# Two-layer decoder trunk in split float32: the layer loop written out, the first loads reordered, the position table written from 8 rows

## The reference

```
h = h + 0.5 * swiglu(rms_norm(h, ffn1_norm[l]), ffn1_gate[l], ffn1_up[l], ffn1_down[l])
h = h + token_mixing(rms_norm(h, mix_norm[l]), ...)
h = h + 0.5 * swiglu(rms_norm(h, ffn2_norm[l]), ffn2_gate[l], ffn2_up[l], ffn2_down[l])
```

## Time and profile before

| what | value |
|---|---|
| median of the runs shown | 1044.88 us |
| profiled execution, device time | 1045.52 us |
| its span, first to last instruction | 1043.7 us |
| PE busy | 1016.2 us (97%) |
| DVE, ACT, POOL busy | 709.4, 495.9, 85.5 us |
| mean granted TensorE clock | 0.994 |
| DMA | 183.46 MB, 176 GB/s over the span |

### The profile page before, as it was taken

One profiled execution on the slowest core, in us unless ns is written; L12 is line 12 of the kernel. 1 busy time (PEld: TensorE's weight loads), 2 busy tenths in 40 slices (PEclk: granted clock), 3 DMA queues, 4 the chain that ended last, 5 costly groups with the idle time before them and its releaser, 6 DMA issues.

```text
span 1043.7 us, 19491 instructions
## 1 busy us (share of the span) xinstructions
PE 1016.2 (97%) x7096; PEld 926.3 (89%) x7096; DVE 709.4 (68%) x1405; ACT 495.9 (48%) x804; POOL 85.5 (8%) x120
## 2 busy tenths in 40 slices
PE   7999999999989999999989999999999999999996
PEld 7999999989867999999989999999897689999996
DVE  5766666679676766666577666666896767666665
ACT  6544444564545444444355444445745454444442
POOL 1000000010551000000010000000015500000000
PEclk9999999999999999999999999999999999999999
DMA  8855555544533555555446555554453446555541
GB/s 318 304 183 189 187 185 182 176 161 138 188 108 136 191 192 188 189 186 181 143 134 211 183 183 185 187 187 142 143 202 122 133 151 221 188 192 183 181 141 41
DMA packets 35873, 183.46 MB, mean 176 GB/s; under 512 B 3952, under 2 KB 6000, under 8 KB 21360
## 3 DMA queue, kind: packets, MB, share of 16 engines
q1 hardware_dynamic: 35824, 182.83, 52.3%
HBM read 180.19 MB, written 2.62 MB: 175 GB/s over the span
## 4 chain that ended last, share of the span: by engine, by line
PE 91%; issue 3%; DVE 3%; ACT 1%; POOL 1%; DVEq 0%; POOLq 0%; ACTq 0%
PE ps L516 28%; PE ps L518 27%; PE ps L517 27%; DVE wlo L916 1%; PE ps L527 1%; PE ps L528 1%; PE ps L531 1%; PE ps L694 1%; PE ps L706 1%; PE ps L555 1%; PE ps L685 1%; PE ps L681 1%; DVE wlo L922 0%; DVE X L964 0%; PE ps L563 0%
## 5 line engine op out<-in xcount | busy, mean ns | idle before, releaser
L516 PE MATMUL ps<-xhi,whi 128*128 128x256 f32 x1600 | 454.0, 284 | 0.0
L518 PE MATMUL ps<-xhi,wlo 128*128 128x256 f32 x1600 | 452.2, 283 | 0.0
L517 PE MATMUL ps<-xlo,whi 128*128 128x256 f32 x1600 | 451.8, 282 | 0.0
L516 PEld LDWEIGHTS ps<-xhi,whi 128*128 128x128 f32 x1600 | 306.0, 191 | 5.7 <-issue 2.0
L517 PEld LDWEIGHTS ps<-xlo,whi 128*128 128x128 f32 x1600 | 306.0, 191 | 3.8
L518 PEld LDWEIGHTS ps<-xhi,wlo 128*128 128x128 f32 x1600 | 306.1, 191 | 0.0
L916 DVE TENSOR_TENSOR wlo<-raw,whi 128x1024 fp32r<-128x1024 f32 (+2 forms) x224 | 261.1, 1203 | 9.2 <-ACT whi L313 7.2
L313 ACT CAST whi<-raw 128x1024 fp32r<-128x1024 f32 (+2 forms) x224 | 219.3, 1028 | 29.4 <-PE ps L518 27.2
L922 DVE TENSOR_TENSOR wlo<-raw,whi 128x1024 fp32r<-128x1024 f32 (+1 forms) x112 | 131.5, 1174 | 97.7 <-ACT whi L317 97.7
L346 ACT ACTIVATE sig<-hg 128x256 f32<-128x256 f32 x88 | 36.9, 419 | 273.0 <-DVE hg L981 273.0
L516 PE MATMUL ps<-whi,hhi 128*128 128x512 f32 x352 | 139.8, 397 | 0.4 <-DVE hlo L993 0.4
(11 more groups left out here) (146 smaller groups left out, 907.1 us busy)
## 6 DMA issues: line engine op xcount, KB each, us to landing
raw<-stream SPq DMA_DIRECT2D x112, 1024.0 KB, 5.2
raw<-stream SPq DMA_DIRECT2D x112, 512.0 KB, 3.6
table<-feat SPq DMA_DIRECT2D x1, 1536.0 KB, 12.7
cst<-consts SPq DMA_DIRECT2D x1, 1088.0 KB, 12.9
X<-x SPq DMA_DIRECT2D x2, 512.0 KB, 5.6
bias<-table SPq DMA_DIRECT2D x1, 1024.0 KB, 6.2
out<-feat SPq DMA_DIRECT2D x4, 256.0 KB, 2.1
fgain<-final_gain SPq DMA_DIRECT2D x1, 512.0 KB, 8.0
```

Source lines behind the costliest of these rows:

```text
L516: nc.tensor.matmul(out_, a[0], b[0], start=start, stop=False)
L517: nc.tensor.matmul(out_, a[0], b[1], start=False, stop=False)
L518: return nc.tensor.matmul(out_, a[1], b[0], start=False, stop=stop)
```

## The change

**Layer loop.** It is written out on PE, ACT, DVE and POOL. The list `NEXT` gives the splits at the end of each FFN: at the end of layer 0's ffn2 they are the front and back of layer 1's chunk 0 and, on ACT, the front of its chunk 1, as at the end of ffn1. The separate gains copy is gone; `gains_all` is read in its place.

**Order of the first loads.** X block 0, the identity, the gains, X block 1, then chunk 0's front in two halves on semaphores of their own, chunk 1's front, both backs, and only then the one-hot matrix, `rel_bias` and the other constants. `lead` takes the place of `first` in up(0) of layer 0: gate products first, with DVE splitting that half, then up products.

**Position table.** PE makes one product of 8 rows x 384 (two matmuls) after up(0), in bank 3; POOL prepares its operands ahead of its first `power`. ACT copies it after step(0), and PE waits for that copy before down(0). SP does reload(1) first, then waits for the table, writes it with each of the 8 source rows read 128 times, and waits for that write as before. ACT and DVE no longer wait for it in the mixing. Before the first transposes PE runs ten matmuls on zeros.

```diff
+NEXT = [(MIX_USED[0], MIX_USED[1][0]), ((FRONT, UNIT), FRONT)] * (DEPTH - 1) + [(MIX_USED[0], MIX_USED[1][0]), ((0, 0), 0)]
...
-        rbhi, rblo = (wlo[0:NBUCKET, 1, i * NH * P:(i + 1) * NH * P].rearrange("p (h q) -> p h q", h=NH)
-                      for i in range(2))
-        onehot_r = wlo[0:NBUCKET, 1, FRONT:FRONT + TAB]
-        tab = feat[:, 0:12, :].rearrange("p a t -> p (a t)").rearrange("p (h y) -> p h y", h=NH)
+        onehot_r = ohi[0:NBUCKET, 0:2, :].rearrange("p a t -> p (a t)")[:, 0:TAB]
+        rbhi, rblo = (olo[0:NBUCKET, 0, i * NH:(i + 1) * NH] for i in range(2))
+        tab = prT[0:NH, 0, :]
...
+        def front_arrivals(l, k, i=0):
+            return arrivals(l, k, i) if k % 2 else (l * (LC // 2) + i + k // 2) * 16
...
-            sp.dma_start(cst[:, 0:C_RB], consts[:, 0:C_RB]).then_inc(table_in, 16)
-            sp.dma_start(rb, rel_bias).then_inc(rb_in, 16)
-            for b in range(NB):
-                sp.dma_start(X[:, b, :], x[:, b, :]).then_inc(x_in[b], 16)
+            sp.dma_start(X[:, 0, :], x[:, 0, :]).then_inc(x_in[0], 16)
+            sp.dma_start(cst[:, 0:C_OH], consts[:, 0:C_OH]).then_inc(id_in, 16)
             sp.dma_start(gains_all[:, :, :], gains).then_inc(gain_in, 16)
+            sp.dma_start(X[:, 1, :], x[:, 1, :]).then_inc(x_in[1], 16)
+            for g in range(2):
+                sp.dma_start(raw[:, 0, g * UNIT:(g + 1) * UNIT], stream[0, :, g * UNIT:(g + 1) * UNIT]).then_inc(lead_in[g], 16)
...
-            for s in range(2):
-                load_front(s, 0)
-                load_back(s, 0)
+            load_front(1, 0)
+            load_back(0, 0)
+            load_back(1, 0)
+            sp.dma_start(onehot, consts[0:NBUCKET, C_OH:C_RB]).then_inc(table_in, 16)
+            sp.dma_start(rb, rel_bias).then_inc(rb_in, 16)
             sp.dma_start(cst[:, C_CM:NC], consts[:, C_CM:NC]).then_inc(const_in, 16)
-            sp.wait_ge(tab_sb, NH)
-            sp.dma_start(table.rearrange("h (p y) -> p h y", y=TAB), tab).then_inc(table_out, 16)
             reload(1)
+            sp.wait_ge(tab_sb, 1)
+            sp.dma_start(table.rearrange("h (p y) -> h p y", y=TAB), tab.unsqueeze(1).to_broadcast([NH, P, TAB])
+                         ).then_inc(table_out, 16)
             sp.wait_ge(table_out, 16)
             skew = table[:, P - 1:P - 1 + P * (TAB - 1)].rearrange("h (p y) -> p h y", y=TAB - 1)
             sp.dma_start(bias[:, :, :], skew[:, :, 0:S]).then_inc(bias_in, 16)
...
-            with pool.Fori(0, DEPTH) as l:
+            pool.wait_ge(rb_in, 16)
+            pool.wait_ge(table_in, 16)
+            nc.gpsimd.tensor_copy(rbhi, rb).then_inc(rb_set, 1)
+            nc.gpsimd.tensor_copy(onehot_r, onehot).then_inc(rb_set, 1)
+            pool.wait_ge(rb_set, 2)
+            nc.gpsimd.tensor_tensor(rblo, rb, rbhi.bitcast(F32), ALU.subtract).then_inc(rb_set, 1)
+            for l in range(DEPTH):
...
-            def norm(n, g, l, ahead=None):
+            def norm(n, g, l, first=False):
                 squares(n, 0)
...
                     if k % 2 == 0:
                         act.wait_ge(xt_mm, n * (KT // 2) + (k // 2 + 1))
                     nc.scalar.mul(xhi[:, k, :], ps[:, 4 + k // 2, S * (k % 2):S * (k % 2) + S],
-                                  gain[:, g + k:g + k + 1]).then_inc(xhi_out, 1)
-                if ahead is not None:
-                    split_front(l, ahead)
+                                  gains_all[:, l, g + k:g + k + 1]).then_inc(xhi_out, 1)
+                if first:
+                    act.wait_ge(lead_in[1], 16)
+                    nc.scalar.copy(whi[:, 0, UNIT:FRONT], raw[:, 0, UNIT:FRONT]).then_inc(hi_front, 2)
                 squares(n, 1)
+                if first:
+                    split_front(l, 1)
...
                 step(0)
+                if (l, phase) == (0, 0):
+                    act.wait_ge(tab_mm, 1)
+                    nc.scalar.mul(tab, ps[0:NH, TABB, 0:TAB], 1.0 / SCALE).then_inc(tab_sb, 1)
                 step(1)
                 with act.Fori(0, NF // 2 - 2) as i:
                     step(2, i)
                     step(3, i)
-                step(NF - 2, front=MIX_USED[0][0] if phase == 0 else 0)
-                step(NF - 1, back=MIX_USED[0][1] if phase == 0 else 0, front=MIX_USED[1][0] if phase == 0 else 0)
+                (front, back), after = NEXT[l * 2 + phase]
+                step(NF - 2, front=front)
+                step(NF - 1, back=back, front=after)
...
-                act.wait_ge(table_out, 16)
...
-            for h in range(NH):
-                act.wait_ge(tab_mm, h + 1)
-                nc.scalar.mul(tab[:, h, :], ps[:, h % 4, 0:TAB], 1.0 / SCALE).then_inc(tab_sb, 1)
             act.wait_ge(gain_in, 16)
-            with act.Fori(0, DEPTH) as l:
-                split_front(l, 0)
-                act.wait_ge(x_ready, l * (3 * 2 * NB) + 1)
-                nc.scalar.copy(gain[:, :], gains_all[:, bass.ds(l, 1), :].rearrange("p a n -> p (a n)")
-                               ).then_inc(gain_set, 1)
-                act.wait_ge(gain_set, l + 1)
-                norm(l * 3, G_FFN1, l, 1)
-                split_back(l, 0)
+            for l in range(DEPTH):
+                norm(l * 3, G_FFN1, l, first=l == 0)
+                if l == 0:
+                    split_back(l, 0)
...
+            def lead(n):
+                for g in range(2):
+                    if g == 0:
+                        pe.wait_ge(lead_hi, 1)
+                    else:
+                        pe.wait_ge(hi_front, 2)
+                    for k in range(KT):
+                        if g == 0:
+                            pe.wait_ge(xhi_out, n + k + 1)
+                        nc.tensor.matmul(ps[:, g, 0:S], whi[:, 0, g * UNIT + k * P:g * UNIT + (k + 1) * P], xhi[:, k, :],
+                                         start=k == 0, stop=False)
+                    pe.wait_ge(w_front, g + 1)
+                    for k in range(KT):
+                        nc.tensor.matmul(ps[:, g, 0:S], wlo[:, 0, g * UNIT + k * P:g * UNIT + (k + 1) * P], xhi[:, k, :],
+                                         start=False, stop=False)
+                for k in range(KT):
+                    pe.wait_ge(xlo_out, n + k + 1)
+                    last = [nc.tensor.matmul(ps[:, g, 0:S], whi[:, 0, g * UNIT + k * P:g * UNIT + (k + 1) * P], xlo[:, k, :],
+                                             start=False, stop=k == KT - 1) for g in range(2)]
+                return last
+            def relative_bias():
+                pe.wait_ge(rb_set, 3)
+                nc.tensor.matmul(ps[0:NH, TABB, 0:TAB], rbhi, onehot_r, start=True, stop=False)
+                nc.tensor.matmul(ps[0:NH, TABB, 0:TAB], rblo, onehot_r, start=False, stop=True).then_inc(tab_mm, 1)
...
                     if f == 0:
+                        if (l, phase) == (0, 0):
+                            lead(0)[1].then_inc(front_done, 1)
+                            relative_bias()
+                            return
...
                 up(1)
+                if (l, phase) == (0, 0):
+                    pe.wait_ge(tab_sb, 1)
                 down(0)
...
-            for h in range(NH):
-                pe.wait_ge(rb_set, 3 if h < NH // 2 else 4)
-                if h >= 4:
-                    pe.wait_ge(tab_sb, h - 3)
-                nc.tensor.matmul(ps[:, h % 4, 0:TAB], rbhi[:, h, :], onehot_r, start=True, stop=False)
-                nc.tensor.matmul(ps[:, h % 4, 0:TAB], rblo[:, h, :], onehot_r, start=False, stop=True).then_inc(tab_mm, 1)
+            pe.wait_ge(nc2_set, 1)
+            for i in range(10):
+                nc.tensor.matmul(ps[:, WARMB, 0:S3], nc2[:, 0:P], nc2[:, :], start=True, stop=True)
+            pe.wait_ge(id_in, 16)
             pe.wait_ge(ones_set, 1)
-            with pe.Fori(0, DEPTH) as l:
+            for l in range(DEPTH):
...
+                if first:
+                    dve.wait_ge(lead_in[0], 16)
+                    nc.vector.tensor_copy(whi[:, 0, 0:UNIT], raw[:, 0, 0:UNIT]).then_inc(lead_hi, 1)
+                    dve.wait_ge(lead_hi, 1)
+                    nc.vector.tensor_tensor(wlo[:, 0, 0:UNIT], raw[:, 0, 0:UNIT], whi[:, 0, 0:UNIT].bitcast(F32),
+                                            ALU.subtract).then_inc(w_front, 1)
                 for t in range(KT):
                     if t % 2 == 0:
                         dve.wait_ge(xhi_out, n * KT + (t + 2))
                     nc.vector.scalar_tensor_tensor(
                         out=xlo[:, t, :], in0=ps[:, 4 + t // 2, S * (t % 2):S * (t % 2) + S],
-                        scalar=gain[:, g + t:g + t + 1], in1=xhi[:, t, :].bitcast(F32),
+                        scalar=gains_all[:, l, g + t:g + t + 1], in1=xhi[:, t, :].bitcast(F32),
                         op0=ALU.mult, op1=ALU.subtract).then_inc(xlo_out, 1)
+                    if first and t == KT // 2 - 1:
+                        split_front(l, 0, halves=(1,))
                 mean(n, 0)
```

(50 more changed lines are left out.)

## The result

The changed kernel takes 1068.97 us (median of 4 executions, 1067.49 to 1070.59), the kernel before 1045.10 beside it (4 executions). The ratio is 1.0227, 95% interval 1.0207 to 1.0247: slower by 2.3%. The profiled execution took 1070.59 us with a span of 1068.8, against 1045.52 and 1043.7 before. The 25.1 us between the spans are what has to be explained.

A forecast was written before the change was run, and what follows sets the result against it. PE bounds the kernel (91% of the span). 1045.52 - 5.5 (passage) + 1.7 (start) + 22.9 (stall) + 1.5 (lower clock) = 1066.1, less 0.64: 1065.5 us; range 1040 to 1071.

The forecast's parts named there:

- The passage: Layer 0 to layer 1: early splits save 3.95 us of PE waiting and 1.54 us of lower clock, together 5.5 us.
- The start: Before down(0): PE's wait for ACT's table copy gives the early start back, clock falls; +1.7 us, bounds -3 and +3.
- The write: Position table's write out of 8 neighbouring partitions: two ways at 53.6 GB/s, 31.3 us, bounds 7.3 and 60.7.
- the sharing by fours: In the table's write: neighbouring source partitions share one of 16 parallel ways by fours, so 8 rows have two.
- From the bias read to chunk 4's front: SP's loads behind the table's write: chunk 4's front lands 10.9 us after the bias read is issued.
- The stall: Before up(4): PE stands still from 49.6 to 72.5, 22.9 us, because chunk 4's weights wait behind the table's write.
- The lower clock after the stall: From up(4) on: PE runs 1.5 us longer at the lower clock after standing still.
- the source doesn't matter: Rival for the table's write: 7.3 us whatever the source partitions, total 1041.1 us; chance 0.12.
- only the number of engines matters: Rival for the table's write: 8 of 16 DMA engines, 9.3 us, total 1041.9 us; chance 0.11.
- one way: Rival for the table's write: all 8 rows share one way, 60.7 us, total 1095 us; chance 0.05.

The follow-up runs named there:

- the kernel with all of it mended: Changed kernel with table rows in every fourth partition, table in bank 6, chunks 4 to 7 issued before SP's wait, one-hot/bias first, back split behind residuals: 1034.82 us.
- the rows by two, four and sixteen: Changed kernel with the table's 8 source rows in every second, fourth or sixteenth partition instead of 0 to 7: 1051.79, 1045.32 and 1051.69 us.

## Why the prediction was right

The forecast was 1065.5 us and slower; measured were 1068.97. Its mechanism held: the write out of 8 neighbouring partitions runs at the rate of two ways, SP's wait passes its landing on to the weights, and PE stands still before up(4). One link was missing without changing the number. The forecast had only SP's wait between the write and the weights, and the loads would have stood behind the write in the same queue even without it (1060.32 us). By its own steps:

- *The passage, 5.5 us.* 4.63. The lower clock went as forecast (3.91 us for the 32 products, forecast 3.88). The waiting shrank to 2.88 us and not to 2.05. The price I took from the earlier trace rows was that of a passage whose last step splits only 8 columns on DVE. Here DVE splits a full back (start, duration, line, operands, idle before) between PE's last products and the residual:

```profile
549.82 1.23 DVE L970 TENSOR_TENSOR wlo<-raw,whi 128x1024 fp32r<-128x1024 f32 x1 [2.03 <-ACT whi L334]
550.96 2.48 DVE L1023 SCALAR_TENSOR_TENSOR X<-ps,X 128x512 f32<-128x512 f32 x4
```

  With that split moved behind (in the kernel with all of it mended, where the residual begins at 516.81, ahead of the last product), the waiting was 2.14 us. I had put "under PE's last down products" for it without asking what stands behind it on DVE. That kernel's other edits lie at the start. That the loop itself costs nothing was right (kernel before with only its loop written out).
- *The start, +1.7.* down(0) began at 28.52 (forecast 28.0), with 3.40 us of idleness on ACT's copy ahead of it (3.4) and a fall of the clock (1.47 us, from the start of down(0) to that of down(1): 10.20 against 8.73; forecast 1.5). Inside it, the bias values landed at 17.1 and not 15.5:

```profile
17.24 0.23 POOL L307 CAST olo<-cst 32x8 fp32r<-32x8 f32 x1 [16.36 <-DMA cst<-rel_bias]
17.42 0.49 POOL L308 CAST ohi<-cst 32x384 fp32r<-32x384 f32 x1
...
18.15 1.06 POOL L291 TENSOR_TENSOR rstd<-ms,mhalf 128x1 f32<-128x1 f32 x2
```

  The last back ahead of them, issued at 5.04, took 11.6 us and landed at 16.6, not at 15.4; why, no run here shows. The three POOL operations took 0.9 us (1.0). But the two powers behind them took 1.06 us and not the 1.98 of the earlier trace rows, which made good more than half of the late landing. That `hg` came at 23.02, near the 22.3 of the forecast (25.08 before), is in this part luck: two misses against each other.
- *The write, 31.3 us.* 34.9. The number of ways was right, the rate of one was not: 24 GB/s instead of the 26.8 that 429 over 16 gives. This is the largest part of the miss, 3.6 us. One reason that I gave for the value doesn't hold: 31.3 is not the middle of the bounds by ratio. That middle of 7.3 and 60.7 is 21.1 us, and the sum with it would have been 1055.3. What carried the value was the sharing by fours alone, which no row of before shows; the rows by two, four and sixteen bore it out afterwards.
- *From the bias read to chunk 4's front, 10.9 us.* 9.75 (63.42 to 73.17). 0.6 of the 1.2 us lies before the front's issue (1.42 us after the bias read's instead of 2.04) and 0.6 between issue and landing (8.33 against 8.9). No weight load was in flight here when the bias read was issued, which may be why; no run shows it.
- *The stall, 22.9 us.* 25.38. up(4) at 75.60 instead of 72.5: 0.5 from the later issue, 3.6 from the write, 1.15 back from the front, 0.2 for the two halves of the splits (2.4 us instead of 2.2).
- *The lower clock after the stall, 1.5 us.* up(4) to down(3) took 8.29 us instead of 5.74, so 2.55. I had taken the price of a 3 us wait for one of 25 us. After the short wait before down(0) the price was 1.47 us; after the long one the granted clock was still 0.50 from 75 to 80 us.
- *Not in the sum:* the mixing stages, -1.92 and +1.32 us.

Up to the first marker the forecast's start, stall and clock give 26.1 us where 30.31 were measured, 4.2 us too little. The passage gained 0.9 us less than forecast, and the later stages gave 0.6 us back: 4.2 + 0.9 - 0.6 = 4.5, the distance between the profiled execution (1070.59) and the 1066.1 of the sum. The rivals "the source doesn't matter" (7.3 us) and "only the number of engines matters" (9.3 us) were refuted by the 34.9 us of the write, and so was "one way" (60.7 us); the rows by two show besides that the place of the rows sets the rate while everything else stays. I gave the four cases 0.71, 0.12, 0.11 and 0.05 with only the arithmetic of ways to part them; no row of before could have done more.

## What to carry to other kernels

A transfer out of few partitions is to be priced by how many parallel ways these partitions reach, and not by its bytes or its descriptors alone: spreading eight rows over partitions 0, 4, ..., 28 turned 34.9 us into 10.6. A slow transfer also holds up what stands behind it in two ways, through the wait of the engine that issued it and through its own queue, so put it in a queue that carries nothing urgent, and issue the urgent transfers ahead of it. And when a step is moved ahead of a passage, look at what stands behind it on the same engine: the price of a similar passage holds only if the sizes are the same.

## What was not expected of the hardware

- Eight ways gave 182 GB/s, nearly as much per way (22.8) as two did (23.9). That a load in SP's queue takes 9.67 us merely to be issued behind the write was new to me.
- The mixing stage takes 126.2 to 126.4 us or 128.1 to 128.3 in these profiled executions, with one between (126.8, layer 1 of the kernel before). In six of the ten both layers have the short length. A long one is layer 0's in the kernel before, and layer 1's in the changed kernel, in the rows by four and in the mended kernel. In each of the four the granted clock falls within the stage. In the kernel before it is layer 0's (columns as above; then the changed kernel's, layer 1's):

```profile
313.00:317.00 4.00, 4.00 (x18) 2.96 (x15) 1.62 (x10) 3.07 (x10) 1.78 (x4) 0.75 0.25 101
```

```profile
848.00:852.00 4.00, 3.87 (x22) 2.29 (x23) 2.07 (x13) 0.10 (x1) 1.04 (x3) 0.65 0.88 339
```

  The same stages of the other kernel, layer 1's before and layer 0's after, have none:

```profile
815.00:851.00 36.00, 33.57 (x203) 26.14 (x202) 26.21 (x64) 19.10 (x43) 12.12 (x16) 1.00 0.43 147
```

```profile
330.00:366.00 36.00, 33.67 (x203) 26.25 (x202) 25.82 (x62) 19.32 (x42) 12.86 (x16) 1.00 0.43 147
```

  The stage's code is the same for both layers, so it doesn't decide alone. Nor does what PE did just before: in each of the four the fall follows a place where PE is busy for only 2.4 to 2.5 us of 4, and in layer 0 of the changed kernel PE is as little busy there (2.48 of the 4 us from 338 on) and the clock stays at 1.00. Executions of one kernel differ as well: the kernel before ran at a mean clock of 0.993 to 0.997. What decides stays open. It moves the time by up to 1.9 us a layer, as much as the 0.2% that can be told apart, and it gives the greater part of the 2 us between the 6.65 of the loop alone and the 4.6 of its passage.
- With the write in ACT's queue the executions spread over 6.8 us, with the mended kernel over 2.5. How the two queues' packets fall beside each other may be the reason; no run here shows it.
